# Inverse of 32x32 triangular blocks in a two-block transformer kernel: the third set moves from VectorE to GpSimd

## What is computed

```
# SSD, per chunk of 128 tokens
acum = cumsum(dt_c * A)
seg = acum[i] - acum[j]
lmat = exp(where(causal, seg, -inf))
scores = einsum('bcihn,bcjhn->bcijh', C_c, B_c) * lmat
y = einsum('bcijh,bcjhp->bcihp', scores, xdt) \
    + einsum('bcihn,bchpn->bcihp', C_c, h_prev) * exp(acum)

# GDN, per chunk
kk = einsum('bchik,bchjk->bchij', k_beta, kc) * decay
tmat = eye(Q) + where(strict, kk, 0.0)
sol = triangular_solve(tmat, rhs, lower=True, unit_diagonal=True)
u, w = sol[..., :V], sol[..., V:]
# then, chunk after chunk
v_new = u - w @ S
S = S * exp(g) + k_dec.T @ v_new
```

## Time and profile before

| | us |
|---|---|
| median of 3 runs | 2527.21 |
| lowest, highest | 2524.04, 2527.45 |
| the profiled execution | 2524.44 |
| its span | 2522.6 |
| SSD output stage in it | 549 to 662.5 |

### The profile page before, as it was taken

How to read it: one execution, slowest core, us unless ns; L and a number is a source line. 1 busy time by engine, 2 the same in 40 slices (tenths; PEclk the granted TensorE clock), 3 DMA queues, 4 the chain that set the end, 5 groups by cost and what they waited for, 6 DMA issues and landing times.

```text
span 2522.6 us, 31195 instructions
## 1 busy us (share of the span) xinstructions
PE 2317.0 (92%) x12406; PEld 1844.6 (73%) x12406; DVE 1368.2 (54%) x2165; ACT 1015.7 (40%) x1687; POOL 148.7 (6%) x108
## 2 busy tenths in 40 slices
PE   3899899978679898999998899999999899999997
PEld 2788787734468786888887658888888657888885
DVE  8567684469667634544455654434344564434445
ACT  3445556623442734233255354223234354322222
POOL 0000000000000010000031301000002301000002
PEclk8989999976699998999999999999999999999998
DMA  6232524621354322222232102222323101232322
GB/s 241 101 117 101 192 84 145 206 51 38 73 147 104 141 95 82 98 96 100 93 107 75 59 1 93 100 99 94 101 88 112 59 26 59 92 101 92 100 95 81
DMA packets 124481, 248.34 MB, mean 98 GB/s; under 512 B 58097, under 2 KB 58865, under 8 KB 123569
## 3 DMA queue, kind: packets, MB, share of 16 engines
q1 hardware_dynamic: 106320, 234.02, 27.9%
q10 hardware_dynamic: 18016, 12.33, 1.6%
HBM read 221.13 MB, written 25.17 MB: 98 GB/s over the span
## 4 chain that ended last, share of the span: by engine, by line
PE 76%; DVE 10%; ACT 5%; DMA 4%; issue 3%; SPq 1%; ACTq 1%; POOL 0%; DVEq 0%
PE bank L1264 18%; PE bank L1265 18%; PE bank L1266 18%; PE bank L942 4%; DMA raw<-in_s_qkvx 2%; DVE cacc L2071 2%; PE bank L1096 2%; PE bank L1426 1%; PE bank L1415 1%; PE bank L941 1%; PE bank L392 1%; PE bank L394 1%; PE bank L393 1%; DMA modw<-in_w_mod 1%; DVE smal L2612 1%
## 5 line engine op out<-in xcount | busy, mean ns | idle before, releaser
L1718 ACT ACTIVATE whi<-raw 128x1024 fp32r<-128x1024 f32 (+1 forms) x267 | 277.8, 1041 | 926.7 <-PE bank L1266 922.3
L1264 PE MATMUL bank<-ahi,whi 128*128 128x512 f32 x1152 | 454.7, 395 | 8.9 <-DVE alo L2475 5.9
L1265 PE MATMUL bank<-alo,whi 128*128 128x512 f32 x1152 | 450.6, 391 | 0.0
L1266 PE MATMUL bank<-ahi,wlo 128*128 128x512 f32 x1152 | 450.3, 391 | 0.0
L2355 DVE TENSOR_TENSOR wlo<-raw,whi 128x1024 fp32r<-128x1024 f32 (+1 forms) x267 | 327.5, 1226 | 133.4 <-ACT whi L1718 133.0
L1264 PE MATMUL bank<-bhi,whi 128*128 128x512 f32 x736 | 286.6, 389 | 0.0
L1265 PE MATMUL bank<-blo,whi 128*128 128x512 f32 x736 | 286.4, 389 | 0.0
L1266 PE MATMUL bank<-bhi,wlo 128*128 128x512 f32 x736 | 286.3, 389 | 0.0
L1264 PEld LDWEIGHTS bank<-ahi,whi 128*128 128x128 f32 x1152 | 217.7, 189 | 60.0 <-issue 11.3
L1265 PEld LDWEIGHTS bank<-alo,whi 128*128 128x128 f32 x1152 | 217.7, 189 | 46.1 <-issue 1.4
L1266 PEld LDWEIGHTS bank<-ahi,wlo 128*128 128x128 f32 x1152 | 217.6, 189 | 45.6
(11 more groups left out here) (428 smaller groups left out, 3744.3 us busy)
## 6 DMA issues: line engine op xcount, KB each, us to landing
raw<-in_s_gu SPq DMA_DIRECT2D x88, 512.0 KB, 3.2
raw<-in_s_qkvx SPq DMA_DIRECT2D x34, 512.0 KB, 4.8
late_modw<-in_w_mod SPq DMA_DIRECT2D x32, 512.0 KB, 3.8
raw<-in_s_up SPq DMA_DIRECT2D x32, 512.0 KB, 3.3
raw<-in_s_down SPq DMA_DIRECT2D x32, 512.0 KB, 3.2
raw<-in_s_dn SPq DMA_DIRECT2D x32, 512.0 KB, 3.3
raw<-in_s_win SPq DMA_DIRECT2D x24, 512.0 KB, 3.2
raw<-in_s_zg SPq DMA_DIRECT2D x16, 512.0 KB, 4.0
```

The costliest lines, as they stand in the source:

```text
L1264: pe.matmul(out, w_hi, x_hi, start=start, stop=False)
L1265: pe.matmul(out, w_hi, x_lo, start=False, stop=False)
L1266: return pe.matmul(out, w_lo, x_hi, start=False, stop=stop)
L1718: act.activation(whi[u % 2][:, 0:width[u + 2] * P], raw[u % 2][:, 0:width[u + 2] * P], ACT.Identity).then_inc(hi_ready, 1)
```

## The change

Set 2 goes to GpSimd. Its XB and XT get buffers of their own at 164 and 168 KB, over the first two chunks of `xtm`, which are read last by the tenth `xwb` (GpSimd waits for `xw_ready` 10, reached in the stage before). GpSimd zeroes XB[2], waits for the blocks of UB[2], does the two copies, all 31 steps and the last copy, and only then waits for the stores and zeroes DT0. VectorE does only sets 0 and 1, the same 124 instructions on them, now over 24 pairs (one or two steps behind each, 31 in all) and so over chunks 0 to 2; chunk 3 has none. SP stores set 2 before sets 0 and 1 and before it loads DT0; its waits for both counts become 64.

```diff
-        XB = [at(f"XB{s}", kb, (P, 1024)) for s, kb in enumerate((148, 152, 140))]
-        XT = [at(f"XT{s}", kb, (P, 1024)) for s, kb in enumerate((140, 144, 144))]
+        XB = [at(f"XB{s}", kb, (P, 1024)) for s, kb in enumerate((148, 152, 164))]
+        XT = [at(f"XT{s}", kb, (P, 1024)) for s, kb in enumerate((140, 144, 168))]
...
+        def three(t):
+            return t[:, :].rearrange("p (i c) -> p i c", i=32)
+        def inverse_start(eng, ch):
+            eng.memset(XB[ch][:, :], 0.0).then_inc(inv_done[ch], 1)
+            eng.wait_ge(inv_done[ch], 1)
+            eng.memset(XB[ch][:, 0:1024:33], 1.0).then_inc(inv_done[ch], 1)
+        def eliminate(ch, st):
+            upper = ch != 1
+            k = 31 - st if upper else st
+            i0, i1, c0, c1 = (0, k, k, 32) if upper else (k + 1, 32, 0, k + 1)
+            u, xm = three(UB[ch]), three(XB[ch])
+            ni, nc_ = i1 - i0, c1 - c0
+            tmp_ = TB[ch][:, 0:ni * nc_].rearrange("p (i c) -> p i c", i=ni)
+            return (tmp_, u[:, i0:i1, k].unsqueeze(2).broadcast_to((P, ni, nc_)),
+                    xm[:, k, c0:c1].unsqueeze(1).broadcast_to((P, ni, nc_)), xm[:, i0:i1, c0:c1])
...
+            store_mixed()
...
-            sp_.wait_ge(xb_stored, 32)
-            sp_.wait_ge(xv_stored, 32)
+            sp_.wait_ge(xb_stored, 64)
+            sp_.wait_ge(xv_stored, 64)
-            store_mixed()
...
-                if t == 3:
-                    sp_.wait_ge(xb_stored, 64)
-                    sp_.wait_ge(xv_stored, 64)
...
-            chains = ((0, slice(0, P), True), (1, slice(0, P), False), (2, slice(0, P), True))
...
-                pair, m = (0, 1) if n < 16 else (2,), n % 16
-                if n == 16:
-                    dve.wait_ge(xb_stored, 32)
-                    dve.wait_ge(xv_stored, 32)
-                if m == 0:
-                    for ch in pair:
-                        inverse_start(ch)
-                    for ch in pair:
-                        dve.wait_ge(ub_loaded[chains[ch][0]], 512)
-                    if n == 16:
-                        r = slice(64, P)
-                        after(dve.tensor_copy(three(XT[2], r), UB[2][r, :].rearrange("p (i c) -> p c i", i=32)))
-                        after(dve.tensor_copy(UB[2][r, :], XT[2][r, :]))
-                for s in (2 * m, 2 * m + 1):
-                    if s < 31:
-                        for ch in pair:
-                            t, col, row, dst = eliminate(ch, s)
-                            dve.wait_ge(inv_done[ch], 2 + 2 * s)
-                            dve.tensor_tensor(t, col, row, ALU.mult).then_inc(inv_done[ch], 1)
-                        for ch in pair:
-                            t, col, row, dst = eliminate(ch, s)
-                            dve.wait_ge(inv_done[ch], 3 + 2 * s)
-                            dve.tensor_tensor(dst, dst, t, ALU.subtract).then_inc(inv_done[ch], 1)
-                if m == 15:
-                    for ch in pair:
-                        x, r, upper = chains[ch]
+                if n == 0:
+                    for ch in (0, 1):
+                        inverse_start(dve, ch)
+                    for ch in (0, 1):
+                        dve.wait_ge(ub_loaded[ch], 512)
+                for st in range(31 * n // 24, 31 * (n + 1) // 24):
+                    for ch in (0, 1):
+                        t, col, row, dst = eliminate(ch, st)
+                        dve.wait_ge(inv_done[ch], 2 + 2 * st)
+                        dve.tensor_tensor(t, col, row, ALU.mult).then_inc(inv_done[ch], 1)
+                    for ch in (0, 1):
+                        t, col, row, dst = eliminate(ch, st)
+                        dve.wait_ge(inv_done[ch], 3 + 2 * st)
+                        dve.tensor_tensor(dst, dst, t, ALU.subtract).then_inc(inv_done[ch], 1)
+                if n == 23:
+                    for ch in (0, 1):
-                        dve.tensor_copy(three(XT[x], r), XB[x][r, :].rearrange("p (c i) -> p i c", c=32)).then_inc(inv_done[ch], 1)
+                        dve.tensor_copy(three(XT[ch]), XB[ch][:, :].rearrange("p (c i) -> p i c", c=32)).then_inc(inv_done[ch], 1)
...
-                    inverse_steps(8 * ci + hp)
+                    if ci < 3:
+                        inverse_steps(8 * ci + hp)
...
-            pool.wait_ge(xb_stored, 32)
+            pool.wait_ge(xw_ready, 10)
+            inverse_start(pool, 2)
+            pool.wait_ge(inv_done[2], 2)
+            pool.wait_ge(ub_loaded[2], 512)
+            r = slice(64, P)
+            pool.tensor_copy(three(XT[2])[r], UB[2][r, :].rearrange("p (i c) -> p c i", i=32)).then_inc(pool_done, 1)
+            pool.wait_ge(pool_done, 1)
+            pool.tensor_copy(UB[2][r, :], XT[2][r, :]).then_inc(pool_done, 1)
+            pool.wait_ge(pool_done, 2)
+            for st in range(31):
+                t, col, row, dst = eliminate(2, st)
+                pool.wait_ge(inv_done[2], 2 + 2 * st)
+                pool.tensor_tensor(t, col, row, ALU.mult).then_inc(inv_done[2], 1)
+                pool.wait_ge(inv_done[2], 3 + 2 * st)
+                pool.tensor_tensor(dst, dst, t, ALU.subtract).then_inc(inv_done[2], 1)
+            pool.wait_ge(inv_done[2], 64)
+            pool.tensor_copy(three(XT[2]), XB[2][:, :].rearrange("p (c i) -> p i c", c=32)).then_inc(inv_done[2], 1)
+            pool.wait_ge(xb_stored, 64)
...
-            n_pool = [0]
+            n_pool = [2]
```

17 lines of the change are left out of this document (removed).

## The result

The changed kernel takes 2530.79 us (median of 12), beside 2525.35 us of the kernel before (12): a ratio of 1.0027, 95% interval 1.0017 to 1.0037, +6.8 us. The forecast was +1.5 us, with 0.37 on a time within 0.2% of the kernel before and 0.40 on a slower one. The first timing, +0.27%, lies just outside the 0.2%, the second inside, and the two intervals overlap, so the runs do not tell these two kinds apart. The forecast was near; its three terms were not all right. From here "+x us" means a ratio times the time of its kernel before.

The account below looks back on a forecast made before the run. In the SSD output stage VectorE and PE are both near full, neither the bound alone, PE waiting 13.9 us for `wmat`. -15 + 18 - 1.5 = +1.5 us on 2524.4 gives 2525.9; 2.8 more for the median: 2528.7, range 2514 to 2545.

Parts of the forecast that it names:

- Part B: Chunks 0 and 1: GpSimd's SBUF reads take turns with VectorE, so set 2's work comes back: +18 us (0 to +37).
- Rival 1: GpSimd beside VectorE's elimination: turns don't happen, its instructions fit into gaps; B 0 to 2, time 2511 to 2513; chance 0.15.
- rival 2: Chunks 1 and 2: GpSimd's price per element is higher on these short-row, strided operands; 2540 to 2545; chance 0.28.
- Part A: SSD output stage: work leaves VectorE, which alone would be below PE in every chunk; -15 us (-13 to -20).
- the 13.9 us of PE waits: PE's waits for VectorE's `wmat` over the stage would go but for about 1 behind XB's memsets: -13 us.
- The term for the clock: Chunk 2: clock may stay up where waits go, one or two pairs at 1.8 instead of 3.07 us: -2 (0 to -7).
- at 3.07 us a pair there: Sign against A: PE still waiting for `wmat` in chunk 3, or staying at 3.07 us a pair there.
- Part C: SP's queue: set 2's stores leave at about 615, no longer just ahead of the barrier: -1.5 us (-2.6 to 0).
- The cover of the later stores: Sets 0 and 1 stored later, DT0 loads issued by 657 to 658, barrier about 663 or 664: 6 us of cover.
- The profile's signs: Steps stretched from 567, chunks 1, 2, 3 about 40, 24.5, 20 us, `wmat` waits bunched in chunk 1, barrier not waiting for GpSimd.

Follow-up runs that it names:

- the memset run: Changed kernel with GpSimd's 62 two-input instructions on set 2 replaced by memsets of twice the elements, set 2's inverse left out: 0.9938, -15.7 us.
- before, no set 2: Kernel before without the 62 elimination instructions of set 2 on VectorE, its order and queues unchanged: 0.9944, -14.1 us.
- the run without steps: Changed kernel without GpSimd's 62 elimination instructions on set 2; its memsets, copies, stores and loads stay: 0.9962, -9.6 us.
- set 2 late: Against the changed kernel: sets 0 and 1 over the first 16 pairs, set 2 on GpSimd behind the zeroing of DT0, stored last: 1.0000.
- the evenly spread run on VectorE alone: Changed kernel with set 2 back on VectorE in its own buffers, sets 0 and 1 over pairs 0 to 19, set 2 over 20 to 31: 0.9994.
- before + GpSimd: Kernel before plus 62 two-input GpSimd instructions of the elimination's shapes on buffers nobody else uses: 1.0070, +17.7 us.
- balanced, late: Late order with sets 0 and 1 over pairs 0 to 19, set 2 on GpSimd from pair 16, DT0 zeroed behind it: 1.0006.
- changed over 16 pairs: Changed kernel with sets 0 and 1 over the first 16 pairs again, set 2 on GpSimd as changed: 1.0011, +2.8 us.
- the run without inverses: Kernel before without any of the 186 elimination instructions on VectorE; memsets, copies, stores and loads stay: 0.9896, -26.3 us.

## Why the prediction was right or wrong

**The result** is inside the range, but the nearness of 2530.8 to 2528.7 is partly luck: the medians of the kernel before were 2 to 4 us lower than the one I started from, and the difference was +6.8 and +3.3, not +1.5.

**Part B** was right in mechanism, and near in size: +18 forecast, 16.4 (or 12.9) measured for the steps in the changed kernel and 17.7 in the kernel before. Against the memset run the steps cost 22.5 (or 19.0). In VectorE's busy time the whole change is nearly a circle: leaving out set 2's steps takes 18.9 us off it (98.8 in the kernel before, 79.9 in "before, no set 2"), and GpSimd's steps put 16.5 back. Inside it, two things were off and cancelled: the price was 1.65 ns per element where I had 2.09 from the 128x512 instructions, and less was absorbed. GpSimd didn't need 45 to 48 us in turns but 40.5 (565.16 to 605.71), nearly the 39 that the prediction worked out for it alone: VectorE does the waiting, GpSimd hardly any. Its copies did what the earlier trace rows said, VectorE's `wmat` at 562.16 took 2.01 us beside GpSimd's first, and they were priced too low: 2.5 us for the three, where VectorE lost 4.2 to them in the run without steps.

```profile
561.32 2.57 POOL L2661 COPY XT<-UB 64x1024 f32<-64x1024 f32 x1 [16.61 <-DMA UB<-at_scratch]
...
565.16 0.43 POOL L2668 TENSOR_TENSOR TB<-UB,XB 128x31 f32<-128x31 f32 x1
```

**Rival 1** (no turns) and **rival 2** (dearer elements) are both out. GpSimd's 255-element instructions took 0.64 to 0.72 us, as forecast (0.7); the column inputs at a step of 128 bytes cost nothing extra that could be seen. The Trainium skill's rule of 50% more for reads with a step of more than 8 bytes ("GPSIMD Engine Reference", section "Performance pitfalls for Q7 kernels") would have made them 0.18 + 256 x 3.2 ns = 1.0 us, an estimate by the working of the prediction. In a copy a long step did go with a long time: 2.57 us here and 1.95 in "set 2 late" for the transposing copy of 64x1024, 1.13 for the contiguous one behind it.

**Part A** is the step that failed, in its mechanism; how far its size was off is not settled. -15 was forecast. The run without GpSimd's steps has A, C and the copies in it and measured -9.6; the memset run has the same in it and measured -15.7. Taking C as -2, A with the copies is -7.6 by the one and -13.7 by the other, and without the copies, at 2.5 (the prediction) to 4.2 us (VectorE's rows), -10 to -18 as an estimate: from two thirds of the forecast to a little more than it. The failing sentence is that "the 13.9 us of PE waits" would go, and that this is worth 13; 8.1, 4.9 and 6.1 us of them were still there in the three profiles without GpSimd's steps and 5.7 in that with memsets, and in the evenly spread run on VectorE alone 13.1. I took the waits as time to be had, and weighed VectorE's 22 us against PE's 25. But 25 is PE's time at a clock of 0.62; left to itself it goes to 28.4 at 0.50 as well as to 17.4 at 1.00. At the lower level the relief buys nothing below 28.4; at the upper it buys all, but only in a chunk where VectorE has no steps, since with 22 us of work VectorE is the bound again. The term for the clock (-2, 0 to -7) had too small a range, with no room for a loss, and the wrong place: chunk 3, forecast 20 us, was 28.4 and 28.5; across all profiles a chunk 3 without steps took 17.8 to 29.1. The test that the prediction set, PE staying "at 3.07 us a pair there", came out against it. Line 1075, once per pair:

```profile
651.78 0.61 PE L1075 MATMUL bank<-cb 128*128 128x512 bf16 x1
654.85 0.61 PE L1075 MATMUL bank<-cb 128*128 128x512 bf16 x1
```

Whether spreading, which I took as the way to make the relief count, helps it or works against it isn't shown: without set 2's steps the unspread order is at 0.9944, the spread one at 0.9962 and, with memsets on GpSimd, at 0.9938.

**Part C**: -1.5 forecast. From the last pair to the scan's first matmul it was 14.95 us before and 12.9 and 12.75 after. Where set 2's stores were first issued within 1.4 us of the end of the last pair it was 15.0 to 16.6 in every run; where they went at least 3.7 us before it, 12.2 to 13.1, and this holds too for the two runs that keep the late place in SP's list ("before + GpSimd", "balanced, late"). So -2, a little more than forecast; what goes with it is the time of the stores and not their place in the list. The cover of the later stores held: the scan's first matmul waits for DB and C as before, not for DT0.

```profile
684.12 0.65 PE L1131 MATMUL bank<-DB,C 32*32 32x32 f32 x32 [8.29 <-DMA DB<-xv_scratch]
```

**The profile's signs**: first step 565 (forecast 567), end 606 (614), chunk 1 38.6 us (40), chunk 2 26.4 and 22.7 (24.5), chunk 3 28.4 (20). PE's waits for `wmat` were not bunched in chunk 1: 9.1 us of them lay in chunk 0 and 8.2 in chunk 1. The barrier didn't wait for GpSimd.

## What to carry to other kernels

Before moving elementwise work to GpSimd, count its elements in instructions that read SBUF: beside a VectorE whose instructions have two SBUF inputs they come back onto VectorE nearly whole (16.5 of 18.9 us here), and the work is hidden only beside VectorE's idle time, whatever the engine shares say. Before counting PE's waits as gain, ask how long the stretch takes with PE busy throughout at each of its two clock levels; if both are reached, a relief is worth the one or the other. The profiles here suggest that leaving whole stretches free of the other engine's work is better than thinning it out evenly; the times don't show it.

## What the hardware showed that I had not expected

**A busy PE at the lower clock.** In the memset run's chunk 2 PE was busy for 27.69 of 28.41 us and was granted 0.50 throughout; the chunk behind it, with the same PE instructions, was at 0.82 and took 19.52:

```profile
601.91:630.32 28.41, 27.69 (x154) 15.73 (x153) 21.94 (x69) 10.68 (x36) 0.00 (x0) 0.50 0.09 35
630.32:649.84 19.52, 18.46 (x154) 10.45 (x152) 9.98 (x21) 10.93 (x37) 1.92 (x4) 0.82 0.24 73
```

The Trainium skill ("TensorE: Matmul & The Clock Gate", section "What's actually happening") says that the throttled state is the default and that activity releases it; this chunk, busy and at the lower level throughout, doesn't fit with that as the whole rule. What raises the clock stays open. Waits of PE for `wmat` in the chunk ahead are not needed (this run), idleness of VectorE isn't enough (chunk 3 of the changed kernel), and the chance seems better with two chunks free of steps: five of six were up in the three kernels that have two (before without set 2, changed over 16 pairs, set 2 late), two of six where only chunk 3 is free (the changed kernel and its two variants on GpSimd, six profiles), and in the balanced order chunk 3, free of VectorE's steps, stood at 0.56. These are few, and no run sets it deliberately. For the fall there is more: it came with a wait of PE for VectorE in the two places shown above, in the run without steps and in the run without inverses.

**Why the late order doesn't gain** isn't settled either: it has VectorE at 16 and 14 us in the last chunks, yet it is 14 us slower than the same order without set 2. The barrier's 2.8 us is one part; chunk 2 at 0.56 instead of 0.84 another. The profile is the fastest of the twelve and 8 us below their median, so it doesn't show what the usual execution spends, and one profile can't say whether GpSimd's work or chance kept the clock down.
